# RWKV triangular inverse: level products of one step and updates of the step behind it issued as one burst, with new order strings

## What is computed

```python
def step(S, inp):
    w_t, k_t, v_t, a_t, b_t = inp[:5]
    sa = jnp.einsum('dbhij,dbhj->dbhi', S, a_t)
    S = S * w_t[..., None, :] + sa[..., :, None] * b_t[..., None, :] + v_t[..., :, None] * k_t[..., None, :]
    return S, (jnp.einsum('dbhij,dbhj->dbhi', S, inp[5]) if with_out else None)
```

## Time and profile before

| | us |
|---|---|
| median of 3 runs | 2400.82 (2397.12 to 2406.61) |
| profiled execution, its own time | 2408.59 |
| its span, first to last instruction | 2406.8 |
| RWKV steps with an inverse, about | 1300.8 to 1936 of the span |
| PE busy over the span | 2235.9 (93%) |
| granted TensorE clock, mean | 0.978 |

### The profile page before, as it was taken

The page is one execution under the profiler, slowest core; times in us unless marked ns, Lnnn a source line. Parts: engine busy times, 40 slices in busy tenths (PEclk is TensorE's granted clock), DMA queues, the critical chain, the costliest instruction groups (busy, mean ns, idle before and its releaser), DMA issues.

```text
span 2406.8 us, 63796 instructions
## 1 busy us (share of the span) xinstructions
PE 2235.9 (93%) x27583; PEld 1853.0 (77%) x27583; DVE 1054.1 (44%) x2108; ACT 893.5 (37%) x1707; POOL 707.1 (29%) x535
## 2 busy tenths in 40 slices
PE   5998999899999999989997898898889899999998
PEld 3775677788888888878875777777777768888887
DVE  3326666462111111176235566666666625311213
ACT  3435555333121212263223444554455323332333
POOL 0334455303323232203222313222231300344432
PEclk8999999999999999999998999999999979999999
DMA  8124555212122121213350000000000102323231
GB/s 258 53 53 142 177 173 180 66 53 70 54 69 70 53 70 53 70 36 111 104 160 21 3 25 24 24 4 24 25 12 17 40 20 77 99 88 105 87 103 55
DMA packets 172311, 176.30 MB, mean 73 GB/s; under 512 B 26512, under 2 KB 160032, under 8 KB 172064
## 3 DMA queue, kind: packets, MB, share of 16 engines
q1 hardware_dynamic: 171200, 169.48, 22.5%
q10 hardware_dynamic: 864, 3.15, 0.3%
HBM read 161.06 MB, written 11.53 MB: 72 GB/s over the span
## 4 chain that ended last, share of the span: by engine, by line
PE 83%; DVE 7%; ACT 4%; issue 3%; SPq 1%; DMA 1%; POOL 1%; ACTq 0%; DVEq 0%
PE PS L399 40%; PE PS L560 5%; PE PS L1530 5%; PE PS L419 4%; PE PS L1508 2%; PE PS L758 2%; PE PS L739 2%; PE PS L1314 2%; PE PS L1613 2%; PE PS L718 2%; PE PS L1518 2%; PE PS L1694 1%; PE PS L748 1%; PE PS L1125 1%; PE PS L1249 1%
## 5 line engine op out<-in xcount | busy, mean ns | idle before, releaser
L379 POOL TENSOR_TENSOR WL<-RAW,WH 128x1024 fp32r<-128x1024 f32 x160 | 383.6, 2420 | 940.5 <-ACT WH L360 940.5
L399 PE MATMUL PS<-AH,WH 128*128 128x256 f32 (+1 forms) x992 | 350.8, 354 | 3.3 <-DVE AL L2454 2.4
L399 PE MATMUL PS<-AH,WL 128*128 128x256 f32 (+1 forms) x992 | 351.7, 355 | 0.0
L399 PE MATMUL PS<-AL,WH 128*128 128x256 f32 (+1 forms) x992 | 349.1, 352 | 0.0
L360 ACT ACTIVATE WH<-RAW 128x1024 fp32r<-128x1024 f32 x160 | 159.9, 1048 | 273.3 <-PE PS L399 265.7
L399 PE MATMUL PS<-BH,WL 128*128 128x512 f32 (+1 forms) x672 | 239.2, 356 | 0.0
L399 PE MATMUL PS<-BH,WH 128*128 128x512 f32 (+1 forms) x672 | 238.5, 355 | 0.0
L399 PE MATMUL PS<-BL,WH 128*128 128x512 f32 (+1 forms) x672 | 237.6, 354 | 0.0
L399 PEld LDWEIGHTS PS<-AH,WH 128*128 128x128 f32 x992 | 187.8, 189 | 31.5 <-issue 2.6
L399 PEld LDWEIGHTS PS<-AL,WH 128*128 128x128 f32 x992 | 187.0, 188 | 27.1
L399 PEld LDWEIGHTS PS<-AH,WL 128*128 128x128 f32 x992 | 187.4, 189 | 25.3
(11 more groups left out here) (275 smaller groups left out, 4777.4 us busy)
## 6 DMA issues: line engine op xcount, KB each, us to landing
ADW<-l_ada_w SPq DMA_DIRECT2D x40, 1024.0 KB, 5.3
RAW<-l_mlp_up SPq DMA_DIRECT2D x64, 512.0 KB, 4.6
RAW<-l_mlp_down SPq DMA_DIRECT2D x64, 512.0 KB, 4.1
RAW<-l_w_rkv SPq DMA_DIRECT2D x24, 512.0 KB, 5.3
rwkv_scratch<-STG SPq DMA_DIRECT2D x24, 384.0 KB, 3.4
ADA<-l_ada_w SPq DMA_DIRECT2D x4, 2048.0 KB, 12.7
RAW<-l_w_in SPq DMA_DIRECT2D x16, 256.0 KB, 5.5
RAW<-l_w_out SPq DMA_DIRECT2D x16, 256.0 KB, 5.1
```

The costliest lines, as they stand in the source:

```text
L379: e.tensor_tensor(WL[:, s, rows], RAW[:, s, rows], WH[:, s, rows], ALU.subtract).then_inc(w_split[h], 1)
L399: mm = e.matmul(dst, w[:, s, k, n * P:(n + 1) * P], r[:, k, lo:hi], start=(k == 0 and i == 0), stop=(k == KT - 1 and i == 2), skip_group_c ...
```

## The change

1. On PE a round becomes one piece. For each of its four chunks it issues the two level products of n and then the two `product_xit` of v = n - 1 (four quarters of the array in turn); behind the four, the eight `product_xi` of v. Its second piece is empty. The number of matmuls is the same.
2. The one piece waits for `um_ready` of n - 1 and for `xit_ready` of n - 2 ahead of its first matmul. So level products now wait for ACT's copies too. `u_done` comes with the last level product, `inv_done` with the last `product_xi`.
3. Both strings in `SLOT` are new. They place p, c and i pieces differently on every engine.

DVE's, ACT's and POOL's pieces of the inverse are as before.

```diff
-        SLOT = (("pciipcpiicppcicpipipicicpipciipiipiipipciipic"
-                 "pipcpiicippciippiippcipipcpipippipiipicpiiii"),
-                ("ipcipiicpicppipppppiipipiicpiciipciipciipciipciip"
-                 "cicicpcpiicpcpicpicppipcpicippciciicppiicippciii"))
+        SLOT = (("pcicppiicpppicicipicpiicppicpiiciipcpipiciipi"
+                 "pcipiippcpipiipiciicppippppiipiippiicippiiii"),
+                ("ipcipicpcpiipppppppcpciiipciicpiicpipcipipicppipi"
+                 "cipcpcipiicppicipciiciciipcipcpiicppciipciciiiii"))
...
             for n in range(19):
+                v = n - 1
                 if n < 18:
                     e.wait_ge(um_ready, 18 * q + n)
                     if n < 3:
                         e.wait_ge(lta_ready, 3 * q + n + 1)
-                    for i in range(4):
+                else:
+                    e.wait_ge(um_ready, 18 * q + 18)
+                if 3 <= v < 6:
+                    e.wait_ge(xit_init, 6 * q + 2 * (v % 3) + 2)
+                if v > 3:
+                    e.wait_ge(xit_ready, 15 * q + v - 3)
+                for i in range(4):
+                    if n < 18:
+                        u = 4 * (n % 3) + i
                         for cp, t in enumerate(HALVES):
-                            u = 4 * (n % 3) + i
                             o = HALVES[1 - cp] if n >= 3 else t
                             mm = e.matmul(bank(0)[o, i * C:(i + 1) * C], mt(b, u, 0)[t],
                                           XI[t, u, :] if n >= 3 else IDN[t, t], start=True, stop=True,
                                           skip_group_check=True)
-                    mm.then_inc(u_done, 1)
-                yield
-                if n >= 4:
-                    v = n - 1
-                    if n == 18:
-                        e.wait_ge(um_ready, 18 * q + 18)
-                    if v < 6:
-                        e.wait_ge(xit_init, 6 * q + 2 * (v % 3) + 2)
-                    e.wait_ge(xit_ready, 15 * q + v - 3)
-                    for i in range(4):
+                        if i == 3:
+                            mm.then_inc(u_done, 1)
+                    if v >= 3:
                         for cp in range(2):
-                            if v < 15:
-                                product_xi(v, i, cp)
                             mm = product_xit(v, i, cp)
+                for i in range(4):
+                    for cp in range(2):
+                        if 3 <= v < 15:
+                            mm = product_xi(v, i, cp)
+                if v >= 3:
                     mm.then_inc(inv_done, 1)
+                yield
                 yield
```

More of the change, by code:

```diff
@@ L1203, in build @@
         HALVES = (slice(0, 64), slice(64, 128))
-        SLOT = (("pciipcpiicppcicpipipicicpipciipiipiipipciipic"
-                 "pipcpiicippciippiippcipipcpipippipiipicpiiii"),
-                ("ipcipiicpicppipppppiipipiicpiciipciipciipciipciip"
-                 "cicicpcpiicpcpicpicppipcpicippciciicppiciippciii"))
+        SLOT = (("pcicppiicpppicicipicpiicppicpiiciipcpipiciipi"
+                 "pcipiippcpipiipiciicppippppiipiippiicippiiii"),
+                ("ipcipicpcpiipppppppcpciiipciicpiicpipcipipicppipi"
+                 "cipcpcipiicppicipciiciciipcipcpiicppciipciciiiii"))
         def slots(e, pre, inverse, chain):
@@ L1532, in pe_inverse @@
                                           skip_group_check=True)
-                    mm.then_inc(u_done, 1)
-                yield
-                if n >= 4:
-                    v = n - 1
-                    if n == 18:
-                        e.wait_ge(um_ready, 18 * q + 18)
-                    if v < 6:
-                        e.wait_ge(xit_init, 6 * q + 2 * (v % 3) + 2)
-                    e.wait_ge(xit_ready, 15 * q + v - 3)
-                    for i in range(4):
-                        for cp in range(2):
-                            if v < 15:
-                                product_xi(v, i, cp)
-                            mm = product_xit(v, i, cp)
-                    mm.then_inc(inv_done, 1)
+                        if i == 3:
+                            mm.then_inc(u_done, 1)
+                    if v >= 3:
+                        for cp in range(2):
+                            mm = product_xit(v, i, cp)
+                for i in range(4):
+                    for cp in range(2):
+                        if 3 <= v < 15:
+                            mm = product_xi(v, i, cp)
+                if v >= 3:
+                    mm.then_inc(inv_done, 1)
+                yield
                 yield
```

## The result

The changed kernel takes **2453.96 us** (median of 4 runs, 2449.15 to 2460.07), the kernel before 2400.32 us in the same session. The ratio is 1.0212, 95% interval 1.0192 to 1.0231; a second session gave 1.0207 (1.0182 to 1.0233). The forecast was 2425, with a range to 2446: the sign was right, the size was half of what came, and the time lies outside the range. The profiled execution took 2449.15 us around a span of 2447.3, the fastest of its four; that of the kernel before was 8 us slower than its median.

A forecast was written before the change was run, and what follows sets the result against it. PE, busy for 93% of the span, was taken as the bound. Seven even steps at 2.9 (20.3), odd steps at 0 and +4 for steps 1 and 16 gave +24 us, from 2400.8 to 2425 us; range 2394 to 2446.

The forecast's parts named there:

- the net 0 for odd steps: Odd steps: 2.6 us of new waits against 2.5 us that go away, net 0, give or take 1.5 us.
- the +4 for steps 1 and 16: Steps 1 and 16 have fewer fillers: 5 to 6 us of missing cover each, before about 4.5 and 3; together +4.
- The first term: PE work in a round: the busiest quarters carry 16 records before and after, so merging saves 0; 0.93 us either way.
- The period: Shortest time from one merged burst to the next: 1.76 us, 0.93 of it work, so 0.83 us of cover needed.
- The even step: Even steps: new waits of 4.0 us less 1.3 that go, net +2.7, with last rounds' rounding +2.9 us each.
- The places of the list: Places between rounds of an even step where cover falls short and PE waits, +0.2 to +1.0 us each, sum 4.0 us.
- the 1.3 us that were to go: Even step: present idle time of PE expected to vanish in rounds 5 to 7, at L1314 and near round 17.
- The rival for it: Clock falls to its lower level for 20 us in bare rounds of steps 1 and 16, +10 us; slower beyond 2440, chance 0.13.
- The difference carries over unchanged: The profiled execution before lay 8 us over the median; the span's +24 us was applied to the median as it stood.
- Odd steps that win: Rival: longer covers in odd steps remove 2 us each, sum 10 us, 2411 us; within 0.5%, chance 0.20.
- The cheap `product_xi`: Rival: the 16 lone records run at 0.015 us each, round 0.71 us, 42 us less work, 2372 us; chance 0.12.
- The rival that comes nearest: Slower still: lower clock +10 us and odd steps +1.5 each, 45 us in all, 2446 us; beyond 2440, chance 0.13.

The follow-up runs named there:

- three_in_turn: Changed kernel with `product_xi` taken into the mixture too: per chunk two level products, two `product_xit`, two `product_xi`, 48 records in one run; ratio 1.0220.
- before_fed_half: Kernel before with useless matmuls (20, 8 and 24) in PE's waits at the end of the last inverse and the last chain step; 2398.3 us, ratio 0.9978.

## Why the prediction was half of it

Three terms failed, all of them waits or their consequences: the net 0 for odd steps, the +4 for steps 1 and 16, and the clock, which the forecast put at nothing. The first section below is what came as forecast, then each of the three.

**What held.** The first term, 0 for the quarters: 0.93 us a round in every mixture. The period, 1.76 forecast, 1.79 measured, and the 30 us of waits for L1569 (32.2). The even step: +2.9 forecast, +2.97 measured (39.63 to 42.60). By its places: round 4 to 5 idle 1.23 us (1.14 before, with level products ahead of it then); 6 to 7 and 7 to 8 idle 0.54 and 0.53 (forecast 0.7 and 0.6); 11 to 12 idle 0.41 (0.45); the two L1314 in a row idle 0.82 at a distance of 1.44 us (1.0 and 1.49; from the first two records of the first one it is 1.55). At 5 to 6 there are 0.15 us (0.2), but for the mask and not for the copy. Over seven even steps, at the same clock, the two traces of each kernel give +20.7 us; 20.3 was forecast.

That it is so close is in part luck. The places of the list idle 2.9 us more, where 4.0 were forecast; L1680, which waits 0.43 us for DVE's L1797 ahead of round 5's burst, was not on the list. And of the 1.3 us that were to go, which by their own entries add up to 1.2, I find 0.36 us at L1314 and some 0.3 us of short waits. Both sides were too large by about 0.6 us (3.4 us against 4.0, 0.7 against 1.3).

**Odd steps: 0 forecast, +1.3 us each.** At the same clock the six odd steps from 3 to 13 add up to 252.1 us before and 260.1 after, +8 us. The step that failed is "net 0": I set 2.6 us of new waits against 2.5 that go. As means over both traces, waits with a known releaser rose by 0.2 us a step (4.17 to 4.40), waits for nothing visible ("issue") by 0.5 (1.56 to 2.08), and PE's busy time in steps at full clock by 0.6 (36.1 to 36.7). The first agrees with the 0.1 that I had estimated. The other two I had at 0: "issue" I never priced, and busy time I took as equal because the number of changes between kinds of matmul is. Where the 0.6 comes from was not tested.

**Steps 1 and 15 on: +4 forecast, +8 us.** At the same clock step 1 takes 2.7 us more, and the stretch from step 15 to the end of the chain 5.6 us. The step that failed is the missing cover, mis-sized by half: I had counted it in steps 1 and 16 and let step 15 go with the odd steps at 0. Which places make the 5.6 was not taken apart.

**The clock: nothing in the forecast, some 12 us.** By the mean clock of the runs (0.980 before, 0.9735 after, medians of 13 and 8 executions) the changed kernel spends 2 x (1 - 0.9735) x 2454 = 130 us at the lower level, the kernel before 96; 34 us at 0.35 are 12 us. The rival for it named the right mechanism and the wrong place: I looked for it in the bare rounds of steps 1 and 16. In the traces all of it came in steps 2 to 14: 10 and 10 us at the lower level before, 27 and 41 after; step 1 has none in any trace, and from step 15 on the means are equal (26 us). Its price was too high, 0.5 us for each us at the lower level, where the traces show 0.35. The fall at 1354.6 us in step 2 begins in the middle of a wait for XIT between rounds 4 and 5, a place of my own list, as PE's timeline shows:

```profile
1355.14 0.37 PE L1538 MATMUL PS<-XI,MT_ALL 64*64 64x64 f32 x2 [1.44 <-ACT XIT L1569]
```

The clock should have been a term that follows from that list.

Sum: 20.7 + 8 + 8.3 + 12 = 49 us. The two sessions measured 51 and 50 us by the ratio, 53.6 and 53.0 by the medians; the rest of 1 to 4 us stays open. The first three terms are the +37 of the table; only the 12 rest on a mean price and a mean clock.

**"The difference carries over unchanged"** was wrong too. The profiled execution before lay 8 us over its median, the one after 5 us under its own. The second is the clock (116 us at the lower level instead of 130, 5 us); of the first it explains some 3 us (104 instead of 96), and the rest stays open. A single trace is one draw.

**The rivals.** Odd steps that win: they lost. The cheap `product_xi`: refuted twice, by the timeline and by three_in_turn (its bound in the prediction is 0.22 us a round, as its sum of 42 us uses, and not the 0.24 that stands beside it). The rival that comes nearest had a chance of 0.13: odd steps at the bad end (+1.5 each; +1.3 came) and +10 us of clock (12 came), 45 us in all. The Trainium skill (TensorEngine Tiling (Array Packing), Theoretical Speedup) gives up to two times for a dimension of at most 64. From two quarters to four the traces show it, twice the records in the same 0.47 us, and only where all four quarters have the same number of them.

## What to carry to other kernels

Count the work by quarter before merging bursts: if the busiest quarter has the same number of records before and after, the merge shortens nothing (0.93 us a round in all the orders run here), and all that is left is its waits. Two bursts in turn hide each other's copy and mask, while a merged burst waits for the later of both; where a merge is wanted, keep the half that depends on less ahead of the wait (here 21 us at the same clock, and the clock's share on top; even so it stayed 0.6% above two bursts). And price a list of new waits twice: once for their length, and once for the clock that falls behind them. Where PE must wait near such a fall, work of the length of the wait, into a free bank, can pay: 0.2% at the end of the kernel before, nothing that the total shows in step 2 of the changed one.

## What the runs showed of the chip

- **The clock's falls come behind a few of PE's waits, and which of them have one varies from run to run.** Waits of 1.2 to 1.6 us, with a shorter one beside them, went with most falls, in a kernel whose PE is busy for 92%. The Trainium skill (TensorE: Matmul & The Clock Gate, Part 1: The HAM clock gate) says that the throttled state is the default and activity releases it; that agrees with the fed end of before_fed_half (0.80 to 1.00). What I had not expected is its share in a comparison: two traces of the same kernel differ by 10 us through it.
- **PE's waits for "issue" stand a multiple of 256 records apart.** In the changed kernel's rounds 37 waits of over 0.14 us end with nothing visible. Counting PE's records (loads, matmuls and the few of its sequencer) from one to the next gives 256, 512, 768 and so on, within 2, for all but one at 1371.6. The other three traces of the two kernels show the same, with one such exception each. Three in a row in an odd step:

```profile
1683.72 0.28 PE L1669 MATMUL PS<-SS,AR 64*64 64x64 f32 x4 [0.80 <-issue]
...
1687.49 0.33 PE L1538 MATMUL PS<-XI,MT_ALL 64*64 64x64 f32 x4 [0.25 <-issue]
...
1691.15 0.21 PE L1518 MATMUL PS<-XIT,AR 64*64 64x64 f32 x1 [1.10 <-issue]
```

The page lists a queue for instructions with packets of 16 KB (3.33 MB in 203 packets), which is 64 bytes for each of 256. The natural reading is that PE waits there for its next piece of program. It is only a reading, as no run changed it. From step 1 on these waits are 17.8 and 15.7 us in the two traces of the kernel before, 21.0 and 20.8 in the changed one, and most stand in odd steps and in the last stretch. The same step can have 3.5 us of them in one execution and 1.6 in another (step 5 of the kernel before).
